# Spare elements behind the parts of a weight ring: the same instructions on tiles at other addresses modulo 512 bytes

## The chip, the cores and the metric

The kernel runs on one core of one Trainium2 chip. The metric is the time of one execution on the device in microseconds (us); lower is better. Three runs of the kernel before gave 2739.76, 2740.66 and 2744.77 us, median 2740.66 us.

## The reference, cut to what matters

512 tokens of width 1024 in float32 pass through two blocks of two layers each. The first block has a dilated window attention layer and a differential attention layer, the second twice a hybrid mixer (indexed sparse attention, a gated linear recurrence, gates) with a convolutional feed-forward part. Nearly all arithmetic is in the projections:

```python
def dilated_mixer(h, w_in, w_out):
    proj = h @ w_in                 # [512,1024] @ [1024,10240]
    ...
def diff_mixer(h, w_in, ..., w_out, lambda_init):
    proj = h @ w_in                 # [512,1024] @ [1024,4096]
    ...
def hybrid_mixer(x, pos, w_in, gla_w_gate, ..., p_attn, p_gla, w_out, b_out):
    proj = x @ w_in                 # [512,1024] @ [1024,7256]
    ...
    merged = jax.nn.sigmoid(gate_a) * ya + jax.nn.sigmoid(gate_b) * yb
    return merged @ w_out + b_out
def conv_ffn(x, w_up, conv_w, conv_b, w_down):
    u = x @ w_up                    # [512,1024] @ [1024,5632]
    ...
    return (jax.nn.gelu(a) * b) @ w_down
```

## The kernel before

**Precision.** Each projection is done in three passes, `PASSES = ((0, 0), (0, 1), (1, 0))`: weight and activation are each split into a high part (float32 rounded to the fp32r type) and a low part (what is left), and the products high*high, high*low and low*high are added up in a PSUM bank. So each tile of weights stands in SBUF as two parts of 2048 elements per partition, and so do the activations.

**Tiles and ring.** `weight_tiles` cuts every weight matrix into tiles of 8 x 256 or 4 x 512 elements per partition. SyncE loads a raw tile from HBM into one half of `WR` in two transfers. ScalarE copies it to the high part of a slot (lines 2024 and 2028), and GpSimd (2977 and 2979) or VectorE subtracts to get the low part. The slots are a ring of `NS = 3` in `WS`, taken in turn; a few tiles lie in `EX` or in the arena instead (`place` in `Order`, lines 191 to 195). The activations that the projections read are in `UT`, in `AT` (an alias at the arena's start) or in `EA`.

**The matmuls.** In `tensor`, a step "mm" runs the three passes over the contraction blocks `kk` of one tile and one output block. Every matmul loads a stationary operand of 128 x 128 and streams a moving operand of 512 or 256 columns past it. There are two orientations:

```python
if by_heads(i):       # 1669: stationary = weights (WS), moving = activations (UT)
    mm = pe.matmul(B[bank][:, :], slot(i, part)[:, c:c + P], act[:, other, kk, :], ...)
elif by_feature:      # 1673: stationary = weights (WS), moving = activations (UT, AT, EA)
    mm = pe.matmul(B[bank][0:c, :], w[part][:, kk, g * P:g * P + c], act[:, other, kk, :], ...)
else:                 # 1676: stationary = activations (UT, AT), moving = weights (WS, EX)
    mm = pe.matmul(B[bank][:, off:off + n], act[:, other, before_k + kk, g * P:g * P + P], w[part][:, kk, :], ...)
```

Lines 1694 (moving `UT`, stationary `AT`) and 1709 (moving `UT`, stationary `WS`) are the same with 256 columns. In fp32r every column is 4 bytes, so a stationary operand is 512 bytes per partition and a moving one of 512 columns 2048 bytes. All pieces that these lines address begin at a multiple of 512 bytes from the start of their part (the one exception is the tile of 88 columns, below). The order of all work is written out by `Order`; no address enters it.

**Where the tiles lie.** `build` allocates `UT`, `WS`, `WR`, `CT`, `SM` and the arena one behind the other, each start rounded up to 32 bytes. `UT` starts at 16512. `UT`, `WS` and `WR` have sizes that are multiples of 512 bytes, `CT` has 906 elements (3624 bytes), `SM` 3072 bytes; `AT`, `AF`, `AR`, `MF`, `EX` and `EA` lie at multiples of 512 bytes from the arena's start.

Of the kernel before, what the change touches and what calls it, by code (L numbers as in the profile page):

```python
# [7 lines left out]
F32R = mybir.dt.float32r  # L8
# [5 lines left out]
P = 128  # L14
# [3 lines left out]
KC = 8  # L18
# [17 lines left out]
C_TAB = 906  # L36
# [12 lines left out]
NS = 3  # L49
# [879 lines left out]
def build(nc, ap, out):  # L929
    with ExitStack() as ctx:  # L930
        def sb(name, shape, dt=F32):
            return ctx.enter_context(nc.sbuf_tensor(name, shape, dt))
# [5 lines left out]
            return Tally(sem(name))  # L938

        UT = sb("UT", [P, 2, KC, T], F32R)  # L940
        WS = sb("WS", [P, NS, 2, KC * 256], F32R)
        WR = sb("WR", [P, 2, KC * 256])
        CT = sb("CT", [P, C_TAB])
        SM = sb("SM", [P, 768])

        base = -(-nc.sbuf_base // 32) * 32
# [15 lines left out]

        IDN = CT[:, C_ID:C_ID + 128]
        MHALF, SQ, RS, ST, MV, SA = 0, 16, 32, 64, 200, 232
# [10 lines left out]
        def arr(o, *shape):  # L975
            return view(AR[:, o:o + math.prod(shape)], shape)
# [494 lines left out]
        def slot(i, part):  # L1471
            _, k, n, _ = tiles[i]
            s = place[i]
            if s < NS:
                return WS[:, s, part, 0:k * n]
            if s > NS:
# [19 lines left out]
        def S2(n, c, w):  # L1496
            return fat(6144 + 1024 * (n % 3) + 512 * c, w) if n % 3 < 2 else MF[:, 512 * c:512 * c + w]

        def small2(n, kind, c):

            o = QT + 16 * (n % 4) + {"max": 0, "sum": 2, "weight": 4}[kind] + c
            return SM[:, o:o + 1]
# [116 lines left out]
        def tensor():  # L1619
# [3 lines left out]
            for kind, *a in order.steps:  # L1623
# [313 lines left out]
                elif kind == "totals":  # L1937
# [5 lines left out]
                    for h in range(4):  # L1943
                        mm = pe.matmul(B[k][:, h * 8 + 2 * b:h * 8 + 2 * b + 2], la[:, b, h * P:h * P + P],
                                       CT[:, C_CI:C_CI + 2], start=True, stop=True)
                    if b == NB - 1:
                        mm.then_inc(total_mm.sem, 1)

                elif kind == "decayed_keys":
                    l, b = a  # L1950
                    pe.wait_ge(*before["kdec", l, b])
                    pe.matmul(B[4 + b % 2][:, :], CT[:, C_LM:C_LM + P], la[:, b, :], start=True,
                              stop=True).then_inc(kdec_mm.sem, 1)
# [422 lines left out]
        def vector():  # L2376
# [3 lines left out]
            def tt(out_, x, y, op):  # L2380
                return ve.tensor_tensor(out_, x, y, op)  # L2381

            ve.memset(SM[:, MHALF:MHALF + 16], -0.5).then_inc(half_set, 1)
            for kind, *a in order.steps:
# [175 lines left out]
                elif kind == "rope_table":  # L2560
# [5 lines left out]
                    tt(arr(oANG, 4, 8), arr(oPOS, 4).unsqueeze(2).to_broadcast([P, 4, 8]),  # L2566
                       CT[:, C_INV:C_INV + 8].unsqueeze(1).to_broadcast([P, 4, 8]), ALU.mult).then_inc(dve_step, 1)
                    ve.wait_ge(dve_step, V.of())
# [36 lines left out]
                elif kind == "scores2":  # L2605
# [5 lines left out]
                    for c in range(2):  # L2611
                        x = ve.tensor_tensor_reduce(S2(n, c, w), B[4 + c][:, 0:w], CT[:, C_CM + 512 - w:C_CM + 512],
                                                    -0.125, -GONE, ALU.add, ALU.min, small2(n, "max", c))
# [76 lines left out]
                elif kind == "forbid":  # L2690
                    l, b = a
                    w = P * (b + 1)
                    ve.wait_ge(dots_added.sem, dots_added.at[l, b, 7])
                    tt(WK[:, w - P:w], WK[:, w - P:w], CT[:, C_KM:C_KM + P], ALU.add).then_inc(dve_step, 1)
                    V.of()
# [557 lines left out]
```

## Time and profile before

| | |
|---|---|
| median of three runs | 2740.66 us (2739.76 to 2744.77) |
| span of the profiled execution, first to last instruction | 2738.5 us |
| TensorE matmul busy | 2691.3 us, 98% |
| TensorE weight load busy | 2152.9 us, 79% |
| VectorE, ScalarE, GpSimd busy | 45%, 38%, 42% |
| TensorE's share of the chain that ended last | 95% |
| granted TensorE clock, mean | 0.998 of full speed |
| the 16 DMA engines busy | 34% on the loads' queue |

The busy time of a matmul is modelled with its drain (a matmul of 512 columns counts as some 390 ns), and the drains of a stream overlap. So the time from one matmul to the next isn't the mean in a group's row; it is read from an unbroken piece of the chain: its length divided by its number of matmuls. A piece that ends in a wait has one drain in it, a piece that is followed at once by other matmuls has none.

### The profile page before, as it was taken

How to read it: one execution, taken by the hardware profiler on the slowest of the kernel's cores; microseconds unless marked ns; L12 is line 12 of the kernel's file. 1: busy time of each engine (PE TensorE's matmuls, PEld its weight loads, DVE VectorE, ACT ScalarE, POOL GpSimd, SP SyncE). 2: the span in 40 equal slices, each digit the busy share in tenths (PEclk: the TensorE clock that was granted, in tenths of full speed). 3: DMA queues.
4: the chain of work that ended last, by engine and by line, in shares of the span. 5: the costliest groups of instructions: out<-in, count | busy, mean ns of one | idle time of the engine just before them, and what ended most of it. 6: DMA issues, size and time to landing. Idle time of an engine off the chain costs nothing.

```text
span 2738.5 us, 36085 instructions
## 1 busy us (share of the span) xinstructions
PE 2691.3 (98%) x13721; PEld 2152.9 (79%) x13721; DVE 1225.1 (45%) x2468; ACT 1050.0 (38%) x2005; POOL 1139.6 (42%) x894
## 2 busy tenths in 40 slices
PE   8999999999999999999999999999999999999998
PEld 6887878887777877776788888887777678888887
DVE  4434343443556356544236424255654423642426
ACT  3333334353345334344333424233435333342422
POOL 4434343433442443333365444444333336454443
PEclk9999999999999999999999999999999999999999
DMA  5424342432422242224243333324222425233331
GB/s 189 135 85 132 90 135 85 137 111 81 124 78 77 60 139 77 78 85 126 90 162 109 108 93 101 100 68 139 77 78 85 131 85 176 95 111 98 100 92 62
DMA packets 215057, 286.40 MB, mean 105 GB/s; under 512 B 16862, under 2 KB 154562, under 8 KB 214116
## 3 DMA queue, kind: packets, MB, share of 16 engines
q1 hardware_dynamic: 214884, 284.08, 34.1%
q8 instruction: 110, 1.80, 0.3%
q14 instruction: 63, 0.52, 0.1%
HBM read 248.31 MB, written 18.94 MB: 98 GB/s over the span
## 4 chain that ended last, share of the span: by engine, by line
PE 95%; DVE 2%; ACT 1%; issue 1%; POOL 1%; DMA 0%; ACTq 0%; DVEq 0%; POOLq 0%
PE banks L1676 38%; PE banks L1673 29%; PE banks L1669 13%; PE banks L1806 2%; PE banks L1694 2%; PE banks L1733 1%; PE banks L1788 1%; PE banks L1892 1%; PE banks L1709 1%; PE banks L1915 1%; PE banks L1827 1%; PE banks L1965 1%; PE banks L1849 1%; PE banks L1878 1%; PE banks L1773 1%
## 5 line engine op out<-in xcount | busy, mean ns | idle before, releaser
L2979 POOL TENSOR_TENSOR WS<-WR,WS 128x512 fp32r<-128x512 f32 (+2 forms) x676 | 854.4, 1296 | 1057.2 <-ACT WS L2028 1057.2
L1676 PE MATMUL banks<-WS,UT 128*128 128x512 f32 (+1 forms) x3696 | 796.7, 365 | 5.0 <-DVE UT L2381 3.3
L1676 PEld LDWEIGHTS banks<-WS,UT 128*128 128x128 f32 x3696 | 604.3, 189 | 134.2 <-issue 35.2
L1673 PE MATMUL banks<-UT,WS 128*128 128x512 f32 (+1 forms) x2832 | 660.8, 392 | 0.7 <-ACT AR L2210 0.7
L1673 PEld LDWEIGHTS banks<-UT,WS 128*128 128x128 f32 (+1 forms) x2832 | 526.0, 187 | 125.8 <-issue 16.0
L2028 ACT ACTIVATE WS<-WR 128x1024 fp32r<-128x1024 f32 (+1 forms) x344 | 333.3, 1018 | 220.4 <-PE banks L1676 144.3
L1669 PE MATMUL banks<-UT,WS 128*128 128x512 f32 x1536 | 374.9, 398 | 0.0
L1669 PEld LDWEIGHTS banks<-UT,WS 128*128 128x128 f32 x1536 | 284.1, 189 | 65.1 <-issue 6.2
L1676 PE MATMUL banks<-WS,AT 128*128 128x512 f32 x1296 | 308.5, 396 | 0.0
L2977 POOL TENSOR_TENSOR WS<-WR,WS 128x512 fp32r<-128x512 f32 x128 | 180.5, 1441 | 261.3 <-ACT WS L2024 261.3
L1676 PEld LDWEIGHTS banks<-WS,AT 128*128 128x128 f32 x1296 | 242.2, 188 | 58.3 <-ACT WS L2028 0.7
L2381 DVE TENSOR_TENSOR AF<-banks,AF 128x512 f32<-128x512 f32 x128 | 94.2, 788 | 227.5 <-PE banks L1669 227.5
L2914 DVE SCALAR_TENSOR_TENSOR AR<-banks,AR 128x511 f32<-128x511 f32 x84 | 63.0, 750 | 211.7 <-ACT AR L2350 211.7
L2994 POOL TENSOR_TENSOR SM<-SM 128x1 f32<-128x1 f32 (+2 forms) x44 | 47.3, 1075 | 261.6 <-DVE SM L2882 92.8
L2381 DVE TENSOR_TENSOR AR<-AR,banks 128x512 f32<-128x512 f32 x64 | 43.3, 685 | 163.7 <-PE banks L1676 163.7
L2381 DVE TENSOR_TENSOR AR<-AR 128x512 f32<-128x512 f32 (+3 forms) x93 | 98.0, 1054 | 16.3 <-ACT AR L2103 12.9
L2350 ACT ACTIVATE AR<-banks,AR 128x512 f32<-128x512 f32 x84 | 64.9, 772 | 89.2 <-PE banks L1673 79.9
L2483 DVE CUSTOM_DVE_ANT_0 AF<-banks,MF 128x256 f32<-128x256 f32 (+1 forms) x128 | 46.7, 402 | 104.1 <-PE banks L1773 88.0
L1673 PE MATMUL banks<-AT,WS 128*128 128x512 f32 x384 | 88.2, 391 | 0.0
L2024 ACT ACTIVATE WS<-WR 128x512 fp32r<-128x512 f32 x128 | 69.8, 621 | 44.4 <-PE banks L1669 44.4
L1673 PEld LDWEIGHTS banks<-AT,WS 128*128 128x128 f32 x384 | 72.1, 188 | 15.8
L2124 ACT ACTIVATE AF<-banks 128x512 f32<-128x512 f32 (+1 forms) x64 | 36.5, 571 | 110.3 <-PE banks L1788 110.3
(226 smaller groups left out, 2678.3 us busy)
## 6 DMA issues: line engine op xcount, KB each, us to landing
WR<-in_w_in SPq DMA_DIRECT2D x112, 512.0 KB, 3.6
WR<-in_w_up SPq DMA_DIRECT2D x88, 512.0 KB, 3.5
WR<-in_dil_w_in SPq DMA_DIRECT2D x64, 512.0 KB, 3.9
WR<-in_w_down SPq DMA_DIRECT2D x40, 512.0 KB, 3.7
WR<-in_diff_w_in SPq DMA_DIRECT2D x32, 512.0 KB, 3.8
WR<-in_dil_w_in SPq DMA_DIRECT2D x32, 256.0 KB, 3.3
AR<-AF SPq DMA_DIRECT2D x128, 64.0 KB, 2.4
AR<-AF SPq DMA_DIRECT2D x64, 128.0 KB, 2.5
```

Source lines behind the costliest of these rows:

```text
L1669: mm = pe.matmul(B[bank][:, :], slot(i, part)[:, c:c + P], act[:, other, kk, :], start=start, stop=stop)
L1673: mm = pe.matmul(B[bank][0:c, :], w[part][:, kk, g * P:g * P + c], act[:, other, kk, :], start=start, stop=stop)
L1676: mm = pe.matmul(B[bank][:, off:off + n], act[:, other, before_k + kk, g * P:g * P + P], w[part][:, kk, :], start=start, stop=stop)
L1694: mm = pe.matmul(B[c][:, 256 * half:256 * half + 256], w[x][:, kk, (c % 2) * P:(c % 2) * P + P], UT[:, y, kk, 256 * half:256 * half + 256] ...
L1806: mm = pe.matmul(B[ob][:, r:r + 64], fat(7168 + 512 * e + 256 * hh + j * P, P), vj, start=(j == 0), stop=(j == w // P - 1))
L2024: x = se.activation(slot(i, 0)[:, to].rearrange("p (a f c) -> p a f c", f=2, c=32), src, ACT.Copy)
L2028: se.activation(slot(i, 0)[:, v * h:v * h + h], raw(i)[:, v * h:v * h + h], ACT.Copy).then_inc(hi.sem, 1)
L2350: se.activation(d, B[order.bank[i, half][0]][:, :], ACT.Identity, scale=cp[:, 2, f:f + 1], bias=cp[:, 3, f:f + 1]).then_inc(conv_id.sem, 1)
L2381: return ve.tensor_tensor(out_, x, y, op)
L2914: ve.scalar_tensor_tensor(d[:, 1:T], bank[:, 0:T - 1], cp[:, 1, f:f + 1], d[:, 1:T], ALU.mult, ALU.add).then_inc(dve_step, 1)
L2977: ge.tensor_tensor(low, src, high.bitcast(F32), ALU.subtract).then_inc(lo_p.sem, 1)
L2979: ge.tensor_tensor(slot(i, 1)[:, s], raw(i)[:, s], slot(i, 0)[:, s].bitcast(F32), ALU.subtract).then_inc(lo_p.sem, 1)
```

## The change

The rows of `WS` get sixteen more elements (64 bytes) behind each of the six parts, `CT` gets sixteen more at its end. Nothing reads or writes these elements. No instruction is added, removed or moved on any of the five engines; only the addresses in them change.

```diff
         UT = sb("UT", [P, 2, KC, T], F32R)
-        WS = sb("WS", [P, NS, 2, KC * 256], F32R)
+        WS = sb("WS", [P, NS, 2, KC * 256 + 16], F32R)
         WR = sb("WR", [P, 2, KC * 256])
-        CT = sb("CT", [P, C_TAB])
+        CT = sb("CT", [P, C_TAB + 16])
         SM = sb("SM", [P, 768])
```

The starts that follow, in bytes modulo 512:

| | before | after |
|---|---|---|
| `UT` | 128 | 128 |
| `WS`, slot 0 high, low | 128, 128 | 128, 192 |
| `WS`, slot 1 high, low | 128, 128 | 256, 320 |
| `WS`, slot 2 high, low | 128, 128 | 384, 448 |
| `WR`, `CT` | 128 | 0 |
| `SM` | 192 | 128 |
| arena: `AT`, `AF`, `AR`, `MF`, `EX`, `EA` | 192 | 128 |

The text below calls **step** what (start of the stationary operand that is being loaded) - (start of the moving operand that is being streamed) is modulo 512 bytes, in units of 64 bytes. Counted from the addresses in the two built programs, over all pairs of a matmul of these lines and the load that follows it:

| columns, moving, stationary | pairs | step before | step after |
|---|---|---|---|
| 512, `UT`, `WS` | 4223 | 0 (42 others) | 0: 918, 1 to 5: 3277, others 28 |
| 512, `WS`, `UT` | 2329 | 0 | 0: 568, 3 to 7: 1761 |
| 512, `WS`, `AT` | 1283 | 1 | 0: 304, 3 to 7: 979 |
| 512, `AT` or `EA`, `WS` | 574 | 7 | 0: 111, 1 to 5: 463 |
| 512, `EX`, `UT` | 94 | 7 | 0 |
| 512, `EX`, `AT` | 141 | 0 | 0 |
| 256, `WS`, `UT` | 1079 | 0 | 0: 192, 3 to 7: 887 |
| 256, `UT`, `AT` | 378 | 1 | 0 |
| 256, `UT`, `WS` | 192 | 0 | 0: 64, 1, 4, 5: 128 |

## Rows read from the trace of the kernel before

**Rows 1.** The page's first parts: busy times, and granted clock in 40 slices.
```profile
span 2738.5 us, 36085 instructions
...
PE 2691.3 (98%) x13721; PEld 2152.9 (79%) x13721; DVE 1225.1 (45%) x2468; ACT 1050.0 (38%) x2005; POOL 1139.6 (42%) x894
...
PEclk9999999999999999999999999999999999999999
```
**Rows 2.** The page's part 4, chain that ended last, by engine.
```profile
PE 95%; DVE 2%; ACT 1%; issue 1%; POOL 1%; DMA 0%; ACTq 0%; DVEq 0%; POOLq 0%
```
**Rows 3.** Waits of TensorE, longest three: waiter, releaser, total us, times, longest us.
```profile
PE banks L1733 <- DVE AR L2411: 11.0, 3, 8.9
PE banks L1849 <- ACT AF L2202: 5.0, 5, 1.8
PE banks L1806 <- ACT AF L2124: 4.9, 7, 0.7
```
**Rows 4.** Groups by line and shape, matmuls: xcount | busy us, mean ns | idle before.
```profile
L1673 PE MATMUL banks<-UT,WS 128*128 128x512 f32 x2784 | 649.2, 392 | 0.0
L1676 PE MATMUL banks<-WS,UT 128*128 128x512 f32 x2544 | 641.6, 400 | 5.0 <-DVE UT L2381 3.3 <-ACT WS L2028 1.7
L1669 PE MATMUL banks<-UT,WS 128*128 128x512 f32 x1536 | 374.9, 398 | 0.0
L1676 PE MATMUL banks<-WS,AT 128*128 128x512 f32 x1296 | 308.5, 396 | 0.0
L1676 PE MATMUL banks<-WS,UT 128*128 128x256 f32 x1152 | 155.2, 287 | 0.0
L1694 PE MATMUL banks<-UT,AT 128*128 128x256 f32 x384 | 45.7, 278 | 0.0
L1673 PE MATMUL banks<-UT,WS 128*88 128x512 f32 x48 | 11.6, 396 | 0.7 <-ACT AR L2210 0.7
```
**Rows 5.** Chain in order of time, second half: start us, us, what, xcount.
```profile
1339.89 93.17 PE banks L1673 x408
1433.06 22.04 PE banks L1676 x96
1455.10 0.87 PE banks L1733 x8
1455.97 10.96 PE banks L1676 x48
...
1482.50 5.45 PE banks L1694 x48
...
1494.66 8.38 PE banks L1694 x72
1503.04 76.18 PE banks L1673 x336
1579.22 44.80 PE banks L1676 x192
1624.02 87.07 PE banks L1673 x384
...
1799.44 11.51 PE banks L1709 x96
```
**Rows 6.** What matmuls stand in 1339.89:1433.06, by shape.
```profile
L1673 PE MATMUL banks<-AT,WS 128*128 128x512 f32 x192 | 44.1, 391 | 0.0
L1673 PE MATMUL banks<-UT,WS 128*128 128x512 f32 x120 | 27.5, 390 | 0.0
L1673 PE MATMUL banks<-EA,WS 128*128 128x512 f32 x96 | 22.2, 391 | 0.0
```
**Rows 7.** Chain in the first half: pieces of L1669, and the 88-column tile.
```profile
346.81 13.70 PE banks L1669 x60
...
979.09 5.79 PE banks L1673 x24
```
**Rows 8.** Stretch 1500:2000, busy us by engine (x), clock, DMA share, GB/s.
```profile
1500.00:2000.00 500.00, 498.77 (x2290) 401.02 (x2290) 232.16 (x432) 185.78 (x275) 222.97 (x177) 1.00 0.32 96
```
**Rows 9.** What matmuls stand in 1433.06:1466.9, by shape.
```profile
L1676 PE MATMUL banks<-WS,UT 128*128 128x512 f32 x108 | 25.6, 392 | 0.0
L1676 PE MATMUL banks<-EX,UT 128*128 128x512 f32 x36 | 9.0, 393 | 0.0
```

## The prediction

> **What bounds the kernel now.** I read the busy times first: TensorE matmuls are busy 98% of the span, no other engine over 45%, at the full granted clock of 2.4 GHz but for the start [rows 1]. The chain that ended last is 95% TensorE [rows 2]. The longest wait of TensorE is 11.0 us in total and the next two are 5 us each [rows 3], so all its waits are some 1% of the span. A stretch of 500 us from the middle shows TensorE at 498.77 us while VectorE, ScalarE, GpSimd and the DMA engines are all under half [rows 8]. So the time is the number of matmuls times the time from one to the next, and the only thing that an edit without instructions can change by much is that spacing. Work on the other engines may take a little longer or shorter at other addresses; what covers it is their idle half, and the waits of rows 3 are what it costs if the cover is gone.
>
> So the second reading is of the spacing, from unbroken pieces of the chain. 512 columns at 2.4 GHz are 213.3 ns. The pieces show more, and differently, by where the two operands lie [rows 4 to 6]:
>
> - step 0, moving `UT`, stationary `WS`: 76.18/336 = 226.7 ns and 87.07/384 = 226.7 ns [rows 5].
> - step 1, moving `WS`, stationary `AT`: 44.80/192 = 233.3 ns [rows 5]. The same code line with the same columns, 6.6 ns more.
> - step 7, moving `AT` or `EA`: the piece of 408 has 120 matmuls on `UT` and 288 on `AT` and `EA` [rows 6]; (93.17 - 120 x 0.2267)/288 = 229.1 ns.
> - step 0, moving `WS`, stationary `UT`, with some `EX` at step 7 between [rows 9]: (22.04 + 10.96)/144 = 229.2 ns.
> - 256 columns (106.7 ns at 2.4 GHz): 11.51/96 = 119.9 ns at step 0; (5.45 + 8.38)/120 = 115.3 ns at step 1 [rows 5].
> - the 88-column tile, whose pieces are 352 bytes long and so lie at many steps: 5.79 us for 24 with a drain of 0.39 at its end, (5.79 - 0.39)/23 = 234.8 ns at most, start-up included [rows 7].
>
> Each piece is one layer's, beside much the same work of the other engines, and both pieces of step 0 agree to 0.1 ns though they lie in two stretches. I read this as a dependence of the spacing on the step: while a matmul streams, the next stationary operand is read from the same SBUF, and the two streams get in each other's way by an amount that depends on where they stand relative to each other. That it is the step and not another difference of these lines is inferred, since no piece shows the same line at two steps.
>
> **The change, term by term.** The unknown is the spacing at the steps 2 to 6, which hardly occur before. The nearest rows are 229.1 (step 7) and 233.3 ns (step 1), and the 88-column tile lies at 234.8 or under; nothing at 512 columns lies under step 0's 226.7. I take the middle of the two, 231.2 ns, for every displaced pair of 512 columns, with 226.7 and 233.3 as the bounds. The numbers of pairs are in the table on the change.
>
> 1. Moving `UT`, stationary `WS` (lines 1669, 1673): 3305 pairs leave step 0: 3305 x (231.2 - 226.7) = +14.9 us. Line 1669's matmuls stand in shorter runs between other work, and one such run shows 13.70/60 = 228.3 ns already [rows 7]; what is lost there already isn't lost twice: -1536 x 1.6 ns = -2.5 us. Sum +12.4 us; bounds -2.5 and +19.3.
> 2. Moving `WS`, stationary `AT`: 1283 pairs leave step 1. 304 come to step 0: 304 x -6.6 = -2.0 us; 979 to other steps: 979 x (231.2 - 233.3) = -2.1 us. Sum -4.1 us; bounds -8.5 and -2.0.
> 3. Moving `WS`, stationary `UT`: 1761 pairs leave step 0: 1761 x (231.2 - 229.2) = +3.5 us; bounds -4.4 and +7.2.
> 4. Moving `AT` or `EA`: 463 pairs from step 7 to steps 1 to 5, +2.1 ns each, and 111 to step 0, -2.4 ns each: +1.0 - 0.3 = +0.7 us; bounds -1.4 and +1.7.
> 5. 256 columns: 378 pairs come from step 1 to step 0, 378 x (119.9 - 115.3) = +1.7 us. 887 leave step 0; the only displaced row is lower, so I take 118 ns, -1.7 us; bounds 887 x -4.6 = -4.1 us, and +5.9 us if 6.6 ns are added as at 512 columns. Sum 0.
> 6. Moving `EX`, stationary `UT`: 94 pairs come to step 0, -0.2 us.
>
> The sum is 12.4 - 4.1 + 3.5 + 0.7 + 0 - 0.2 = +12.3 us. On the span of 2738.5 us this gives 2750.8 us; the median of the runs is 2.2 us above the span, so 2753 us. With all terms at their lower bounds the sum is about -19 us (2722 us), at their upper about +34 us (2775 us).
>
> What else moves costs nothing. `WR` and the arena start at other addresses, so loads, copies and subtractions run on other alignments. No trace shows their price; from below and above it is bounded by what TensorE waits for now: its named waits are a few 10 us in all, and the tile copies are 1.7 us of them [rows 4]. A GpSimd or ScalarE that took a few per cent longer would stay at half load [rows 8].
>
> **A rule that speaks against this.** The rows show 226.7 ns at step 0 and 233.3 ns at step 1, both above 213.3 [rows 5]. The Trainium skill, page "TensorE: Matmul & The Clock Gate", section "Step-by-step: what each phase is for", says that TensorE has two independent SBUF read ports and that loading the next weights does not steal read bandwidth from the running matmul; the same page gives about 216 ns from matmul to matmul at 512 columns. By that rule no address matters and the sum would be 0. The trace doesn't agree with its 216 ns, and rows with the same columns differ; it doesn't settle whether that comes from the addresses.
>
> **The rivals.**
>
> *No difference, 2741 us.* The spacing hangs on something else that goes with the lines: the order of the operands, the PSUM bank, or whether the stationary operand was written by ScalarE and GpSimd or by VectorE. Then the edit changes nothing that TensorE sees. For it: line 1676 is the dear one in both its forms (229.2 and 233.3), so it may be the orientation and not the step. Against it: line 1673 itself shows 226.7 with `UT` and 229.1 with `AT` and `EA`, which hold other data and are written by other work. The rule of the skill is of this kind.
>
> *Faster, about 2727 us.* `AT` at step 1 is the badly placed tile and the change mends it, while the ring's displacement costs nothing because steps 2 to 6 are far enough apart to keep out of each other's way. Terms 2 and 3 at their lower bounds are -8.5 and -4.4 us, the first is 0 or -2.5, the 256-column term about -2 after the +1.7 of term 5: -13 to -17 us, so 2724 to 2728 us. Its deciding point: with terms 2 to 6 at some -13 us, a displaced pair of term 1 may cost 13/3305, about 4 ns, over step 0 before nothing is left, and there is a gain over 5.5 us only under some 2.3 ns. For it: at 256 columns the displaced row is the cheaper one. Against it: both displaced rows at 512 columns and the 88-column tile are dearer.
>
> *Much slower, about 2790 us.* At a constant step of 2 to 5 the moving stream keeps running into the load behind which it queues, and pays more than at 1 or 7. If a displaced pair costs 10 ns over step 0 (236.7 ns), the terms are +30.5, +1.3, +13.2, +3.3, together +48 us, 2789 us. For it: the 88-column bound of 234.8 ns is the highest that I found, with a load that is a third shorter. Against it: that tile goes through all steps and still stays there.
>
> **How the numbers follow.** The forecast (displaced pairs between 229 and 233 ns, 2745 to 2768 us) gets 0.50, no difference 0.16, faster 0.18, much slower 0.16. What a measurement of this kernel can tell from no change is 0.2%, 5.5 us: the forecast's low end and the first rival together make 0.20 for no difference, faster 0.19, slower 0.61. The range takes in the forecast, the first rival and most of the two outer ones: 2730 to 2790 us.
>
> **What would show it.** In the trace after, the piece of 336 and that of 384 matmuls of line 1673 must be longer than 76.18 and 87.07 us, by some 3.5 ns per matmul on average (a fifth of the pairs keeps step 0): near 77.4 and 88.4 us. The piece of 192 matmuls with stationary `AT`, now 44.80 us, should fall to about 44.2 us, and the 72 of line 1694 rise from 8.38 to 8.6 us. If the three long pieces keep their lengths to 0.1 us, the first rival holds. If 76.18 falls or stays and 44.80 falls to 43.5, the second does. If the difference between the spans lies in TensorE's waits and not in these pieces, the whole reading is wrong, and the other engines' addresses matter after all. A granted clock below the one of rows 1 would have to be taken out first.

## The result and the profile after

The changed kernel is slower: 2761.89 us median of four runs (2759.44 to 2763.10) against 2741.18 us for the kernel before on the same chip, a ratio of 1.0077 with a 95% interval of 1.0065 to 1.0089. In microseconds that is +20.7; the forecast was +12.3, 2753 us, with a range of 2730 to 2790 us.

The page of the changed kernel, span and busy times, beside [rows 1]:

```profile
span 2760.6 us, 36085 instructions
...
PE 2711.7 (98%) x13721; PEld 2155.1 (78%) x13721; DVE 1229.2 (45%) x2468; ACT 1051.2 (38%) x2005; POOL 1148.4 (42%) x894
...
PEclk9999999999999999999999999999999999999999
```

The span grew by 22.1 us and TensorE's busy time by 20.4 us, with the same number of instructions and the same granted clock (0.999 and 0.998 of full speed). VectorE and ScalarE grew by 4.1 and 1.2 us, GpSimd by 8.8 us, on engines that stand still for more than half of the time. TensorE's waits, the answer that [rows 3] are the head of, changed little:

```profile
PE banks L1733 <- DVE AR L2411: 11.8, 3, 9.5
PE banks L1849 <- ACT AF L2202: 5.0, 5, 1.8
PE banks L1806 <- ACT AF L2124: 4.9, 7, 0.7
```

All of them together are 41.4 us against 40.0. So the loss is in the time from matmul to matmul. The chain in order of time, the same pieces as [rows 5] (start us, us, what, number):

```profile
1347.46 94.37 PE banks L1673 x408
1441.83 22.10 PE banks L1676 x96
...
1464.80 11.10 PE banks L1676 x48
...
1504.31 8.82 PE banks L1694 x72
1513.13 77.74 PE banks L1673 x336
1590.87 44.37 PE banks L1676 x192
1635.24 88.83 PE banks L1673 x384
```

The piece of 336 went from 76.18 to 77.74 us (226.7 to 231.4 ns per matmul), that of 384 from 87.07 to 88.83. The piece with stationary `AT` fell from 44.80 to 44.37 us (231.1 ns), and the 72 of 256 columns rose from 8.38 to 8.82.

### The profile page after: what moved, and what is told of

Its sections match the earlier page's. It is cut to its first block, busy times and chain, and to the rows that moved or that the text cites. A ratio compares the mean times of both kernels' runs of the same rounds, so it can differ in the third digit from the quotient of the medians.

```text
span 2760.6 us, 36085 instructions
## 1 busy us (share of the span) xinstructions
PE 2711.7 (98%) x13721; PEld 2155.1 (78%) x13721; DVE 1229.2 (45%) x2468; ACT 1051.2 (38%) x2005; POOL 1148.4 (42%) x894
## 4 chain that ended last, share of the span: by engine, by line
PE 93%; DVE 3%; ACT 2%; issue 1%; POOL 1%; DMA 0%; ACTq 0%; DVEq 0%; POOLq 0%
PE banks L1676 37%; PE banks L1673 29%; PE banks L1669 13%; PE banks L1806 2%; PE banks L1694 2%; PE banks L1733 1%; PE banks L1788 1%; PE banks L1892 1%; PE banks L1915 1%; PE banks L1827 1%; PE banks L1965 1%; PE banks L1878 1%; PE banks L1773 1%; PE banks L1849 1%; PE banks L1776 1%
## 5 line engine op out<-in xcount | busy, mean ns | idle before, releaser
L1673 PE MATMUL banks<-UT,WS 128*128 128x512 f32 (+1 forms) x2832 | 672.1, 396 | 0.7 <-ACT AR L2210 0.7
L1669 PE MATMUL banks<-UT,WS 128*128 128x512 f32 x1536 | 377.7, 399 | 0.0
L1669 PEld LDWEIGHTS banks<-UT,WS 128*128 128x128 f32 x1536 | 283.2, 189 | 67.9 <-issue 6.2
```

## Experiments: is it the ring, and is it the step?

All kernels below have the instructions of the kernel before in the same order and compute the same; they differ only in spare memory. Where a spare tile is added it stands on the line of the tile that follows, so the line numbers stay. The pieces quoted are always the 336 matmuls of line 1673 (moving `UT`, stationary `WS`) and the 192 of line 1676 (moving `WS`, stationary `AT`). "Before" measured 2741.67 us beside the first four of them.

**The ring alone.**

```diff
-        WS = sb("WS", [P, NS, 2, KC * 256], F32R)
-        WR = sb("WR", [P, 2, KC * 256])
+        WS = sb("WS", [P, NS, 2, KC * 256 + 16], F32R)
+        sb("spare", [P, 32]); WR = sb("WR", [P, 2, KC * 256])
```

> Only the six parts of WS are spread; a spare tile of 128 bytes behind the ring puts WR, CT, SM and the arena back on their old addresses modulo 512. Step theory (the spacing of matmuls depends on where the load stands to the moving operand): the ring's displacement is nearly all of the loss, the AT matmuls no longer sit at one step and give back some 2 us, so 2741 + 14 (UT, WS) + 4 (WS, UT) + 1 (AT, EA moving) - 2 (AT stationary) = 2758 us (2752 to 2764); the piece of 336 matmuls near 77.7 us. Rival (addresses of WR, CT and the arena matter, through the other engines or DMA): 2741 to 2745 us, piece of 336 at 76.2.

Measured: 2758.24 us, ratio 1.0063 (1.0050 to 1.0075). The chain of this kernel:

```profile
1508.66 77.74 PE banks L1673 x336
1586.40 44.45 PE banks L1676 x192
```

The piece of 336 is that of the changed kernel to the hundredth. The displaced parts of the ring are 16.6 of the 20.7 us. Most of what is left lies in the matmuls of 256 columns: line 1694 stays at step 1 here and its 72 take 8.38 us, against 8.82 in the changed kernel; from the starts of the single matmuls the 256-column pairs took 2.2 us less here than there.

**Everything but the ring.**

```diff
-        WR = sb("WR", [P, 2, KC * 256])
-        CT = sb("CT", [P, C_TAB])
+        sb("spare", [P, 96]); WR = sb("WR", [P, 2, KC * 256])
+        CT = sb("CT", [P, C_TAB + 16])
```

> The ring is as before; WR, CT, SM and the arena lie at the addresses modulo 512 of the changed kernel (spare tile of 384 bytes behind the ring, 16 elements behind CT). All steps are 0. Step theory: faster by 1283 x 6.6 ns + 574 x 2.4 ns - 378 x 4.6 ns = 8.5 + 1.4 - 1.7 = 8.2 us, 2733 us; the piece of 192 with stationary AT falls from 44.80 to 43.5, the 72 of line 1694 rise from 8.38 to 8.7. Rival (the other engines' addresses are what slowed the changed kernel): 2755 to 2762 us.

Measured: 2735.12 us, ratio 0.9975 (0.9966 to 0.9985), faster than the kernel before. The rival that blames the other engines' addresses falls with this.

**All steps at 0, WR and CT as before.**

```diff
-        SM = sb("SM", [P, 768])
+        sb("spare", [P, 112]); SM = sb("SM", [P, 768])
```

> One spare tile of 448 bytes between CT and SM: the ring, WR and CT as before, the arena at 128 modulo 512 like UT and WS. All steps are 0 and WR and CT are untouched. Step theory: the same 2733 us as with WR and CT moved, within 2 us. If WR or CT matter, the two kernels differ by more.

Measured: 2734.35 us, ratio 0.9970 (0.9960 to 0.9981). It beats both kernels, and agrees with the one above to 0.8 us, so where `WR` and `CT` lie makes no difference that these runs can see. The chain of this kernel:

```profile
1495.43 8.83 PE banks L1694 x72
1504.26 76.19 PE banks L1673 x336
1580.45 43.52 PE banks L1676 x192
```

Line 1676 with stationary `AT` now runs at 43.52/192 = 226.7 ns, the same as line 1673. The difference between the lines was their step and not the orientation of their operands. The 72 matmuls of 256 columns pay for it: 8.38 to 8.83 us.

**The whole ring 64 bytes further.** This puts line 1673 itself at two steps.

```diff
-        WS = sb("WS", [P, NS, 2, KC * 256], F32R)
-        WR = sb("WR", [P, 2, KC * 256])
+        sb("spare0", [P, 16]); WS = sb("WS", [P, NS, 2, KC * 256], F32R)
+        sb("spare1", [P, 112]); WR = sb("WR", [P, 2, KC * 256])
```

> The whole ring lies 64 bytes further, everything else as before. Lines 1669 and 1673 with UT now run at a constant step 1, line 1676 with UT at step 7, all AT and EA matmuls at step 0. This is one line at two steps. Step theory: piece of 336 from 76.18 to 336 x 233.3 ns = 78.4 us, piece of 192 with stationary AT from 44.80 to 43.5; in all 4181 x 6.6 - 2.5 (already lost) - 8.5 - 1.4 = +15 us, 2756 us (2748 to 2765). Rival (the orientation of the operands or the line sets the spacing, not the step): both pieces keep their lengths, 2741 us. Second rival (only changing steps cost, a constant step is as good as another): piece of 336 at 76.2, 2732 to 2741 us.

Measured: 2753.12 us, ratio 1.0044 (1.0031 to 1.0056). The chain of this kernel:

```profile
1508.35 78.39 PE banks L1673 x336
1586.74 43.54 PE banks L1676 x192
```

Both pieces came as the step theory had them (78.4 and 43.5). The two lines have changed places: 233.3 ns for line 1673, 226.8 for line 1676. The same instruction with the same operands costs 6.6 ns more or less by 64 bytes of distance.

**Everything 64 bytes further**, sixteen elements ahead of `UT`: no step changes, all addresses do.

```diff
-        UT = sb("UT", [P, 2, KC, T], F32R)
+        sb("spare0", [P, 16]); UT = sb("UT", [P, 2, KC, T], F32R)
```

> Sixteen elements ahead of UT: every tile lies 64 bytes further, no step changes. Theory (only the relative place counts): span 2738.5 us within 4, pieces 76.18, 44.80, 87.07 and 8.38 us unchanged to 0.1. Rival (it is the address itself: 128 modulo 512 is a good start for a stationary operand, 192 a bad one): UT and WS now lie at 192, so the piece of 336 goes to 78.4 us and the span to 2765 or more.

Measured: span 2741.1 us, one run of 2742.40 us beside one of 2741.94 us for the kernel before (span 2740.6). The chain of this kernel:

```profile
1505.64 76.18 PE banks L1673 x336
1581.82 44.80 PE banks L1676 x192
```

All tiles 64 bytes further, and nothing changes: what counts is where the two operands lie relative to each other.

## Experiments: the curve, its period and the change from step to step

The same edit with 32 and 96, 64 and 64, 48 and 80, 8 and 120 elements ahead of and behind the ring moves the whole ring by 128, 256, 192 and 32 bytes.

> The whole ring 128 bytes further: UT, WS at a constant step 2, WS, UT at 6, WS, AT at 7, AT, WS at 1. If the cost is a smooth function of the step with its least at 0, step 2 costs 233 to 237 ns per matmul (piece of 336: 78.4 to 79.5 us). If each constant step settles at its own value, 226.7 to 237. Piece of 192 with AT at step 7: 229 ns, 44.0 us. Span 2748 to 2775 us. The much-slower rival of the prediction (a constant step of 2 to 5 pays 10 ns or more over step 0): piece of 336 over 79.5 us, span over 2780.

> The whole ring 256 bytes further: UT, WS and WS, UT both at a constant step 4, WS, AT at 5, AT, WS at 3. If the pattern of 512 bytes counts, step 4 is the farthest from 0 and costs 230 to 240 ns (piece of 336: 77.3 to 80.6 us; span 2750 to 2790). If the pattern repeats after 256 bytes, step 4 is as good as step 0: piece of 336 at 76.2 us, WS, AT at 5 like step 1, 44.8 us, span 2738 us.

> The whole ring 192 bytes further. By the values of each constant step so far (0 and 4: 226.7 ns, 1 and 5: 233.3, 2: 232.4, 7: 229.1 ns): UT, WS at step 3 as at 7: piece of 336 at 77.0 us; WS, AT at step 6 as at 2: piece of 192 at 44.6 us; WS, UT at 5 as at 1. Sum over the pairs against before: +7.5 + 9.5 - 1.2 + 1.9 = +18 us, span 2756 us (2752 to 2762). A miss of the pieces by over 0.3 us would show that the repeat after 256 bytes holds only for some steps.

> The whole ring 32 bytes further: UT, WS at step 0.5, WS, AT too. If the cost follows the place smoothly, 229 to 231 ns for both: pieces of 336 near 77.3 us and of 192 near 44.2 us. If the two streams meet in units of 64 bytes, one of the two neighbours' values: 226.7 (76.2 and 43.5 us) or 233.3 (78.4 and 44.8 us). Span 2738 to 2758 us.

The spans were 2764.9, 2738.9, 2751.6 and 2768.5 us (single runs of 2766.24, 2740.20, 2752.86 and 2769.86 us; the kernel before took 2741.94 us beside the first two and 2740.51 beside the last two). The chain of the kernel with the ring moved by 128 bytes:

```profile
691.46 36.40 PE banks L1669 x156
...
1516.91 78.08 PE banks L1673 x336
1594.98 43.95 PE banks L1676 x192
```

By 256 bytes:

```profile
1503.50 76.19 PE banks L1673 x336
1579.69 44.80 PE banks L1676 x192
```

By 192 bytes:

```profile
683.49 36.40 PE banks L1669 x156
...
1507.47 76.91 PE banks L1673 x336
1584.37 44.61 PE banks L1676 x192
...
1716.89 44.80 PE banks L1676 x192
```

By 32 bytes:

```profile
1348.33 95.19 PE banks L1673 x408
...
1514.29 78.41 PE banks L1673 x336
1592.70 44.79 PE banks L1676 x192
```

At 256 bytes nothing is left of the effect: both pieces are those of the kernel before, so the pattern repeats every 256 bytes, and step 4 is step 0. With that the two lines measure one curve together (ns per matmul of 512 columns, each step held constant):

```
step (64 bytes)   line 1673, moving UT, stationary WS   line 1676, moving WS, stationary AT
0, 4              76.18 / 336 = 226.7                    43.52 / 192 = 226.7
0.5               78.41 / 336 = 233.4                    44.79 / 192 = 233.3
1, 5              78.39 / 336 = 233.3                    44.80 / 192 = 233.3
2, 6              78.08 / 336 = 232.4                    44.61 / 192 = 232.3
3, 7              76.91 / 336 = 228.9                    43.95 / 192 = 228.9
```

The two columns come from different code lines, operands and kernels, and agree to 0.1 ns. The curve isn't symmetric (step 1 costs 4.4 ns more than step 3), and half a step is as dear as a whole one. In the kernel moved by 32 bytes the piece of 408 has 288 matmuls that move `AT` or `EA` at step 7.5, half a step below 0, and it took 95.19/408 = 233.3 ns too. So it isn't a smooth valley around 0: the 229 to 231 ns expected for half a step, and the 233 to 237 expected for step 2 if the curve were smooth, both fell.

The table hides one thing. The starts of the single matmuls show that at step 2 they follow a pattern that repeats after some eight (228, 230, 233, 241, 232, 231, 232 ns and so on, 232.4 on average). But the other piece of 192 in the kernel moved by 192 bytes, the same line at the same step 6, alternates between 238 and 229 ns and took 44.80/192 = 233.3. The piece of 156 matmuls of line 1669 in the first half, at step 2 in the kernel moved by 128 bytes and at step 3 in the one moved by 192, took 36.40/156 = 233.3 ns in both, and not 232.4 and 228.9. So steps 2, 3 and 6 have a second, dearer value; which of the two a stream falls into, no run was made to find out. At the steps 0, 0.5, 1, 4 and 5 every long run had the one value.

Two spans missed what was expected. At 192 bytes 2751.6 us is just under the 2752 to 2762: from the starts, the pairs with `UT` moving cost 4.5 us more than before and not 7.5, and the matmuls of 256 columns, for which the expectation had no term, took 3.4 us less. At 32 bytes 2768.5 us is 10 us over the highest that was expected. Of the 30 us over the kernel before, 21.3 are in the pairs with `UT` moving and `WS` stationary, which by themselves already lead over 2758 us; 7.6 come from line 1676 with stationary `UT` at step 7.5, 2.5 from `AT` and `EA` moving, and -2.2 from 256 columns.

**The step changes from tile to tile only.**

```diff
-        WS = sb("WS", [P, NS, 2, KC * 256], F32R)
-        WR = sb("WR", [P, 2, KC * 256])
+        WS = sb("WS", [P, NS, 2 * KC * 256 + 16], F32R)[:, :, 0:2 * KC * 256].rearrange("p s (q n) -> p s q n", q=2)
+        sb("spare1", [P, 80]); WR = sb("WR", [P, 2, KC * 256])
```

> Sixteen elements behind each slot and none between its two parts, arena back on its old address: UT, WS pairs at steps 0, 1 and 2 by slot, and the step changes only from tile to tile, not between the high and the low part of one tile. If each pair costs what its step costs, the pairs of slot 0 run at 226.7 ns, those of slot 1 at 233.3, and the piece of 336 is the mean over the slots, near 77.3 us. If what costs in the changed kernel is the change of step (there even the pairs at step 0 took longer than 226.7), few changes bring the mean clearly under its 77.74 us and the pairs at step 0 back to 227 to 228 ns. Span 2750 to 2758 us.

Measured: span 2752.3 us, piece of 336 (chain of this kernel):

```profile
1509.26 77.38 PE banks L1673 x336
```

Sorted by step from the start times of the single matmuls, the pairs of this piece at steps 0, 1 and 2 took 227.0, 233.2 and 232.4 ns, the values of the curve to 0.3 ns. In the same piece of the changed kernel the pairs at step 0 took 230.6 ns.

**Parts at steps 0 and 1 by turns.** Each slot 64 elements longer, its low part 16 elements further:

```diff
-        WS = sb("WS", [P, NS, 2, KC * 256], F32R)
+        WS = sb("WS", [P, NS, 2 * KC * 256 + 64], F32R)[:, :, 0:2 * KC * 256 + 32].rearrange("p s (q n) -> p s q n", q=2)
```

> Each slot of the ring is 256 bytes longer and its low part begins 64 bytes further; slots start at multiples of 256 bytes. So with UT moving two loads in three are at step 0 (or 4) and one in three at step 1 (or 5), changing after every 8 and 4 matmuls, and the steps 2 and 3 don't occur. If each pair costs what a constant step costs: (2 x 226.7 + 233.3)/3 = 228.9 ns, piece of 336 at 76.9 us. If a change of step starts the settling anew, so that 8 matmuls at step 0 aren't enough to get down to 226.7: about 231 ns, 77.6 to 77.8 us, as much as in the changed kernel, and a span near 2755 us against 2748.

Measured: span 2751.9 us. The chain of this kernel:

```profile
1507.20 77.65 PE banks L1673 x336
```

77.65/336 = 231.1 ns, against 228.9 for a mix of the constant values. So the change of step costs by itself: the pairs at step 0 pay it (230.8 ns over all unbroken pairs with `UT` moving), those at step 1 are even a little cheaper than at a constant step (232.0). In the changed kernel the starts of eight matmuls at step 0 behind four at step 1 are 229, 231, 231, 236, 228, 233, 230 and 227 ns apart: they are down at 227 only at the end of the eight, and then the step changes again.

**64 spare elements in place of 16.**

```diff
-        WS = sb("WS", [P, NS, 2, KC * 256], F32R)
+        WS = sb("WS", [P, NS, 2, KC * 256 + 64], F32R)
```

> The same edit with 64 spare elements (256 bytes) behind each part of the ring in place of 16, CT as before: the parts lie at steps 0 and 4 by turns. The ring moved by 256 bytes as a whole changed nothing, so the pattern repeats every 256 bytes. Theory (only the step modulo 256 bytes counts, also where it changes from part to part): no difference, 2741 us within 0.15%, pieces 76.2, 44.8 and 87.1 us. Rival (any change of address pattern from part to part costs, which would explain the pairs at step 0 that took 231 ns in the changed kernel): piece of 336 at 77 us or more, 2750 us or more.

Measured: 2739.56 us, ratio 0.9999 (0.9990 to 1.0008). The chain of this kernel:

```profile
1501.41 76.18 PE banks L1673 x336
1577.59 44.80 PE banks L1676 x192
```

Six parts spread over other addresses, changing after every few matmuls, and no difference: spare elements behind the parts cost nothing as such. It is the 64 bytes modulo 256.

## Why the prediction was right, step by step

**The bound.** Right. 20.4 of the 22.1 us are in TensorE's busy time, its waits changed by 1.4 us, and the pieces carry the difference.

**The step as the cause.** The prediction called it inferred, since no piece showed one line at two steps. The kernel with the ring moved by 64 bytes shows it, and the one with everything moved shows that the address alone does nothing. What happens between the two operands at a bad distance, which the prediction put as two streams getting in each other's way, stays inferred.

**The price of a displaced pair.** 231.2 ns was taken as the middle of 229.1 and 233.3. The two long pieces of line 1673 averaged 231.4 and 231.3 ns over all their pairs. In the changed kernel the displaced pairs with `UT` moving took 230.5 ns (step 4), 232.1 (steps 1 and 5), 232.6 (step 2) and 230.7 (step 3) where no wait stands between. The middle was near by luck in part: it took steps 2 to 6 for unknown, while steps 4 and 5 are steps 0 and 1. Of 4223 pairs 2013 stand at 0 or 4 and not 918. Had the constant values held for each pair, the piece of 336 (95 pairs at step 0, 64 at 4, 80 at 1 or 5, 64 at 2, 32 at 3) would have taken some 77.1 us, less than forecast; the cost of the changes of step, which the prediction didn't have, filled the gap and somewhat more. Its "fifth of the pairs keeps step 0" is true of all pairs (918 of 4223) and not of this piece, where it is 28%.

**The terms.** From the starts of the single matmuls, over the pairs of the table on the change:

```
term                              forecast   measured
1  UT moving, WS stationary        +12.4      +13.5
2  WS moving, AT stationary         -4.1       -2.5
3  WS moving, UT stationary         +3.5       +4.6
4  AT or EA moving                  +0.7       +1.5
5  256 columns                       0.0       +0.9
6  EX moving, UT stationary         -0.2       -0.2
```

The signs are right (term 5 was put at 0), and terms 1 to 5 each came out 0.8 to 1.6 us too low in the forecast. Terms 1 to 4 together were forecast at +12.5 us and measured +17.1. The displaced pairs in them are not the reason: forecast +14.8, measured +14.5. It is the pairs that stay at step 0 or come to it: forecast -2.3, because they were to run at 226.7 ns, and measured +2.6, because they don't get there when the step changes after every few matmuls. With `UT` moving they took 230.8 ns, with `AT` stationary 229.8. The same cost was already in the 229.2 ns that the prediction read as step 0 with `UT` stationary: a quarter of those matmuls move `EX` at step 7, and in the kernel with all steps at 0 the same two pieces take 21.76 and 10.90 us, 226.8 ns per matmul.

The six are +17.8 us. The forecast had no term for the rest of the growth: the 141 pairs of `EX` and `AT` gave +0.6 us, nearly all in two of them that hold a wait, and over all matmuls of these lines, with those next to other work, the starts give +21.2 us. So the prediction had the cause and the direction, and its sum was too small by 8.4 us of 20.7, with the pairs at step 0 (4.9 us more than forecast) as the largest piece of that. That the time lies in the range of 2730 to 2790 us says little, since the range also took in no difference and a gain; the pieces are the sharper test.

**The pieces.** Forecast 77.4, 88.4, 44.2 and 8.6 us; measured 77.74, 88.83, 44.37 and 8.82.

**The rivals.** *No difference* (orientation, bank or writer of the operand) is refuted: line 1676 at step 0 is as fast as line 1673. By the rule that loading the next weights doesn't take SBUF read bandwidth from the running matmul (the Trainium skill, "TensorE: Matmul & The Clock Gate", "Step-by-step: what each phase is for"), no address would matter. The runs show otherwise: 6.6 ns of 233.3 hang on how far the stationary operand lies from the moving one. Whether it is read bandwidth that is lost, no run shows. *Faster* had its first half right: `AT` at step 1 was badly placed, and moving only `SM` and the arena, so that all steps are 0, gives 0.9970. Its second half, a displaced ring for nothing, was wrong. (Its terms as written add up to -15 to -17 us and not to -13 to -17; nothing hangs on it.) *Much slower* didn't come: no constant step is over 233.4 ns.

**The rest.** "What else moves costs nothing" held: the kernel with only the rest moved agrees with the one in which `WR` and `CT` stay, 2735.12 and 2734.35 us.

## What to carry to other kernels

When TensorE streams without a gap, divide the length of an unbroken piece by its number of matmuls and compare the pieces of different operands: 3% can hide in where the operands lie. For fp32r operands and moving tiles of 512 columns, as here, give stationary and moving tiles the same start modulo 256 bytes, and make every padding a multiple of 256; other types were not measured. A list of tensors whose sizes aren't multiples of that (here a table of 906 elements ahead of the arena) displaces all that follows. When steps are mixed, add the cost of changing between them to the values of the single steps.

## What the runs showed of the hardware

- The time from matmul to matmul at 512 columns of fp32r goes from 226.7 to 233.4 ns with the distance between the two operands modulo 256 bytes; 32 bytes are as dear as 64, and 192 bytes (228.9 ns, in most runs of matmuls) cheaper than 64 (233.3).
- At 256 columns it is the other way, with the same line in the same kernel otherwise: 72 matmuls took 8.38 us at step 1 and 8.83 at step 0, and in the steady part the starts are 113.3 and 120.0 ns apart. Line 1709 shows the same two values, 120.0 in the kernel before and 113.3 with the ring moved by 64 bytes. A kernel with short moving tiles may want another distance.
- A stream has a memory: behind a change of step it takes five to eight matmuls until the spacing of step 0 is reached, and at steps 2, 3 and 6 one and the same step was seen with two steady spacings.
- Even the best step stands 13.4 ns above 213.3 ns, which are 512 periods of a 2.4 GHz clock. None of the kernels here changes that, and what it is stays open. So does the mechanism of the steps. That the reads of the load and of the moving operand meet in parts of the SBUF that alternate within 256 bytes is a guess that would fit the period and the fact that only the relative place counts, but no run shows it; a kernel without the loads wasn't tried.
